# Three homes in turn for the weights of 24 expert blocks, with each weight group issued only when the group two ahead has landed

## The reference, cut to what matters

```python
# 4 groups x 8 experts, each token goes to the best group and to the best 2 experts in it
def expert_block(args):                       # one block of tokens, one expert e
    xe, e = args
    return (jax.nn.silu(xe @ w1[e]) * (xe @ w3[e])) @ w2[e]
# w1[e], w3[e]: 1024 x 512; w2[e]: 512 x 1024; 32 experts in each of 2 layers
```

## Time and profile before

| | |
|---|---|
| median of 3 runs | 1816.01 us (1814.39 to 1816.27) |
| profiled execution | 1816.97 us |
| its span | 1815.2 us |
| PE busy | 1743.2 us (96%) |
| DVE, ACT, POOL busy | 538.1, 525.4, 167.9 us |
| DMA, HBM read | 468.15 MB, 261 GB/s over the span |
| SP's queue of weights | 450.98 MB |

### The profile page before, as it was taken

One profiled execution on the slowest core, in us unless ns is written; L12 is line 12 of the kernel. 1 busy time (PEld: TensorE's weight loads), 2 busy tenths in 40 slices (PEclk: granted clock), 3 DMA queues, 4 the chain that ended last, 5 costly groups with the idle time before them and its releaser, 6 DMA issues.

```text
span 1815.2 us, 23627 instructions
## 1 busy us (share of the span) xinstructions
PE 1743.2 (96%) x9138; PEld 831.6 (46%) x9138; DVE 538.1 (30%) x987; ACT 525.4 (29%) x941; POOL 167.9 (9%) x208
## 2 busy tenths in 40 slices
PE   8999999999999999989999999999999999989898
PEld 4555777455533333333334434685433333333333
DVE  2154555422422231312223004212243232222223
ACT  3245342523322222222223004513432222222213
POOL 2000351110100000000002000320100000000000
PEclk9999999999999999999999999999999999999999
DMA  7210100363499999999994123106399999999995
GB/s 198 93 47 1 48 2 2 109 242 139 150 410 396 421 422 420 421 421 422 420 382 151 48 79 107 47 0 251 123 358 360 421 421 421 421 421 422 421 421 220
DMA packets 98391, 466.48 MB, mean 257 GB/s; under 512 B 23423, under 2 KB 25583, under 8 KB 49178
## 3 DMA queue, kind: packets, MB, share of 16 engines
q1 hardware_dynamic: 87392, 450.98, 62.1%
q0 software_dynamic: 4608, 7.92, 1.2%
q10 hardware_dynamic: 6330, 6.71, 1.2%
HBM read 468.15 MB, written 6.29 MB: 261 GB/s over the span
## 4 chain that ended last, share of the span: by engine, by line
PE 72%; DMA 23%; DVE 2%; ACT 2%; issue 1%; SPq 0%; DVEq 0%; ACTq 0%
PE ps L1132 65%; DMA W<-in_moe_w 23%; PE ps L1341 2%; PE ps L1874 1%; PE ps L1837 1%; ACT MK L900 0%; PE ps L1576 0%; PE ps L1278 0%; PE ps L1145 0%; PE ps L1368 0%; PE ps L1789 0%; DVE gcs L2296 0%; DVE gsn L2327 0%; PE ps L1748 0%; PE ps L1740 0%
## 5 line engine op out<-in xcount | busy, mean ns | idle before, releaser
L1132 PE MATMUL ps<-W,xgT 128*64 128x512 f32 x1984 | 458.2, 599 | 11.6 <-DMA W<-in_moe_w 10.1
L1132 PE MATMUL ps<-HT,W 128*128 128x512 f32 (+2 forms) x896 | 333.9, 533 | 2.8 <-DVE HT L2014 1.4
L1132 PE MATMUL ps<-W,act 128*64 128x512 f32 x992 | 236.6, 611 | 28.4 <-DMA W<-in_moe_w 28.4
L1132 PEld LDWEIGHTS ps<-W,xgT 128*64 128x64 f32 x1984 | 131.2, 136 | 259.8 <-issue 239.7
L1132 PEld LDWEIGHTS ps<-HT,W 128*128 128x128 f32 (+1 forms) x896 | 165.8, 188 | 159.0 <-issue 146.7
L1088 ACT ACTIVATE ysb<-ps 32x512 f32<-32x512 f32 x248 | 146.0, 589 | 262.2 <-PE ps L1132 260.1
L2455 DVE TENSOR_TENSOR XT<-ps,XT 128x512 f32<-128x512 f32 x248 | 159.8, 686 | 170.4 <-PE ps L1132 170.4
L2449 DVE TENSOR_TENSOR act<-ps,sl 128x256 f32<-128x256 f32 x64 | 27.0, 422 | 473.0 <-ACT sl L1081 473.0
L1077 ACT ACTIVATE hs<-ps 128x512 f32<-128x512 f32 x64 | 38.2, 597 | 429.2 <-PE ps L1132 429.2
L1132 PE MATMUL ps<-spread,ysb 64*128 64x256 f32 x992 | 139.8, 401 | 2.7 <-DVE ysb L2475 1.7
L1132 PEld LDWEIGHTS ps<-W,act 128*64 128x64 f32 x992 | 65.8, 139 | 155.3 <-issue 112.9
(11 more groups left out here) (430 smaller groups left out, 1584.8 us busy)
## 6 DMA issues: line engine op xcount, KB each, us to landing
W<-in_moe_w SPq DMA_DIRECT2D x372, 1024.0 KB, 17.5
W<-in_od_w_in SPq DMA_DIRECT2D x6, 2048.0 KB, 8.8
W<-in_ev_w_in SPq DMA_DIRECT2D x3, 2048.0 KB, 7.9
W<-in_xa_wq SPq DMA_DIRECT2D x2, 2048.0 KB, 8.8
W<-in_xa_wo SPq DMA_DIRECT2D x2, 2048.0 KB, 12.8
WY<-in_moe_w SPq DMA_DIRECT2D x4, 1024.0 KB, 8.6
hrows<-hk ACTq DMA_DIRECT2D x8, 512.0 KB, 5.0
HT<-in_moe_w SPq DMA_DIRECT2D x4, 1024.0 KB, 7.7
```

The source lines that it names most:

```text
L1132: return te.matmul(o, l, r, start=first, stop=last)
```

## The change

Three things, and one that makes room for them.

1. **The third place becomes a home.** In the first 12 pairs of a layer (`TURNED = 3 * ROUNDS = 12`), block n uses home n mod 3, where home 2 is HT, WX and WY. Blocks 24 and 25 then stand in homes 0 and 1, and from pair 13 on the old loop with two homes runs.
2. **The order is that of use.** A3 B3, A4 B4, C3, A5 B5, C4, and so on to A24 B24, C23, A25 B25, C24; then the old order. A home is reused after three blocks, so that the wait for PE is for block n-3.
3. **A hold.** Before it issues a group of blocks 4 to 24, SP also waits until the group two ahead of it in this order has landed. A4 waits for B3, the group just before it, and B4 waits for C2, which has long landed. The C groups of blocks 5, 8, ... 23 have no hold, and nothing from A25 on has one.
4. **Semaphores.** Two are needed for home 2 (`third_in`, `second_in`). `brow_in` is counted in `par_in`, and `mem_in` and `gup_in` in one `late_in`, so that PE waits once for 19 small loads where it waited for 14 and then for 5. PE reads the number of pairs after pair 12 and not after pair 1, and adds what the turned part left out to six landing counts.

```diff
-                def up(b, i, readers=0):
+                def up(b, i):
...
+                def hold(signals, place, use):
+                    sp.sem_inc(s["go"], 1)
+                    if place == 2:
+                        sp.wait_ge(s[signals[1]], use * 32 + 32 * (1 + 2 * ROUNDS * L))
+                    else:
+                        sp.wait_ge(signals[0][place], use * 32 + (32 + pairs * 32))
+
+                def turned_up(n, place, use=None):
+                    e = bass.ds(sp.value_load(bei[0:1, bass.ds(n, 1)], min_val=0, max_val=NX - 1), 1)
+                    w1, w3 = (a[k][L][e][0].rearrange("(p k) n -> p k n", p=P) for k in ("moe_w1", "moe_w3"))
+                    for half, signal in enumerate(("hh_half", "hh_done")):
+                        sp.wait_ge(s[signal], n + (pairs * 2 + L))
+                        if use is not None and half:
+                            hold((w2_in, "second_in"), (place + 1) % 3, use[0])
+                        elif use is not None:
+                            hold((w13_in, "third_in"), (place + 2) % 3, use[1])
+                        if place < 2:
+                            up_half(L, place, e, half)
+                        else:
+                            k4 = slice(4 * half, 4 * half + 4)
+                            sp.dma_start(HT[:, k4, :], w1[:, k4, :]).then_inc(s[("extra_in", "third_in")[half]], 16)
+                            sp.dma_start(WX[:, k4, :], w3[:, k4, :]).then_inc(s[("extra_in", "third_in")[half]], 16)
+
+                def turned_down(n, place, use=None):
+                    e = bass.ds(sp.value_load(bei[0:1, bass.ds(n, 1)], min_val=0, max_val=NX - 1), 1)
+                    sp.wait_ge(s["y_done"], n + (pairs * 2 + L))
+                    if use is not None:
+                        hold((wa_in, "extra_in"), (place + 1) % 3, use)
...
-                up(0, 2, readers=1)
-                up(1, 1)
-                down(0, 2, readers=1)
-                down(1, 1)
-                up(1, 2)
-                with sp.Fori(3, trips) as i:
+                turned_up(3, 0)
+                with sp.Fori(1, 2 * ROUNDS) as r:
+                    for q in range(3):
+                        turned_up(r * 3 + (q + 1), (q + 1) % 3, (r + ((q - 1) // 3), r))
+                        turned_down(r * 3 + q, q, r if q < 2 else None)
+                turned_up(2 * TURNED + 1, 1)
+                turned_down(2 * TURNED, 0)
+                with sp.Fori(TURNED + 1, trips) as i:
...
-                            pe.wait_ge(s["par_in"], 16 * (len(PARAMS) - 1))
+                            pe.wait_ge(s["par_in"], 16 * (len(PARAMS) - 1 + 5))
                             te.transpose(ps[:, 2, 0:NPAR], prow[:, :], ident[0:NPAR, 0:NPAR])
-                            pe.wait_ge(s["brow_in"], 16 * 5)
...
-                pair_of_blocks(0, first=True)
-                pair_of_blocks(1, extra=True)
+                for i in range(3):
+                    m = 2 * i
+                    pair_of_blocks(i, ((m % 3, m // 3), ((m + 1) % 3, (m + 1) // 3)), ((m - 1) % 3, (m - 1) // 3), first=i == 0)
+                with pe.Fori(1, ROUNDS) as r:
+                    for p in range(3):
+                        m = 2 * p
+                        pair_of_blocks(r * 3 + p, ((m % 3, (r, m // 3)), ((m + 1) % 3, (r, (m + 1) // 3))), ((m - 1) % 3, (r, (m - 1) // 3)))
+                for place in range(2):
+                    for landing in (wa_in, w13_in, w2_in):
+                        pe.sem_inc(landing[place], 32 * (TURNED - 2 * ROUNDS))
+                pair_of_blocks(TURNED, former=(2, 2 * ROUNDS - 1))
                 pe.wait_ge(s["plan_v"], PLAN_V * (L + 1))
                 trips = pe.value_load(nit[0:1, 0:1], min_val=MIN_TRIPS, max_val=MAX_TRIPS)
-                with pe.Fori(2, trips - 1) as i:
+                last = pe.value_load(nit[0:1, 1:2], min_val=MIN_TRIPS - 1, max_val=MAX_TRIPS - 1)
+                with pe.Fori(TURNED + 1, last) as i:
                     pair_of_blocks(i)
```

More of the change, by code:

```diff
@@ L1846, in add_tiles, with landed, up @@
                     ins.then_inc(s["added"], 1)
-                def up(b, i, between=None, extra=False):
+                def landed(use, per):
+                    return use[0] * (2 * per) + per * (use[1] + 1) if isinstance(use, tuple) else (use + 1) * per
+                def up(b, i, at, between=None):
+                    place, use = at
                     if b == 0:
                         pe.wait_ge(s["xgT_in"], i + (pairs + (L + 1)))
-                    first, third = (HT, WX) if extra else (W8[EXPERT[b]], W8[EXPERT[b] + 1])
-                    if extra:
-                        pe.wait_ge(s["extra_in"], 96 * (L + 1))
+                    first, third = (HT, WX) if place == 2 else (W8[EXPERT[place]], W8[EXPERT[place] + 1])
+                    if place == 2:
+                        pe.wait_ge(s["extra_in"], landed(use, 32) + 32 * 2 * ROUNDS * L)
                     else:
-                        pe.wait_ge(wa_in[b], (i + 1) * 32 + pairs * 32)
+                        pe.wait_ge(wa_in[place], landed(use, 32) + pairs * 32)
                     for k in range(KD):
@@ L1860, in up @@
                             between(k)
-                        if k == 4 and not extra:
-                            pe.wait_ge(w13_in[b], (i + 1) * 32 + pairs * 32)
+                        if k == 4 and place == 2:
+                            pe.wait_ge(s["third_in"], landed(use, 32) + 32 * 2 * ROUNDS * L)
+                        elif k == 4:
+                            pe.wait_ge(w13_in[place], landed(use, 32) + pairs * 32)
                         x = xgT[:, b, k, :]
@@ L1875, in turn_hidden, with down @@
                     ins.then_inc(s["hs_turned"], 1)
-                def down(b, i, bank=6, between=None, extra=False):
+                def down(b, i, at, bank=6, between=None):
+                    place, use = at
                     k0 = i * 2 + (pairs * 2 + b)
                     pe.wait_ge(s["act_in"], k0 + 1)
-                    second = WY if extra else W4[EXPERT[b] + 2]
-                    if not extra:
-                        pe.wait_ge(w2_in[b], (i + 1) * 32 + pairs * 32)
+                    second = WY if place == 2 else W4[EXPERT[place] + 2]
+                    if place == 2:
+                        pe.wait_ge(s["second_in"], landed(use, 32) + 32 * 2 * ROUNDS * L)
+                    else:
+                        pe.wait_ge(w2_in[place], landed(use, 32) + pairs * 32)
                     if bank == 6:
@@ L1909, in next_rows, with pair_of_blocks @@
                         turn_rows(i * 16 + (pairs * 16 + 16))
-                def pair_of_blocks(i, first=False, extra=False, last=False):
-                    up(0, i, extra=extra, between=(lambda k: slots() if k == 4 else None) if first else None)
+                def pair_of_blocks(i, at=None, former=None, first=False, last=False):
+                    at = at or ((0, i), (1, i))
+                    up(0, i, at[0], between=(lambda k: slots() if k == 4 else None) if first else None)
                     if not first:
-                        down(1, i - 1)
+                        down(1, i - 1, former or (1, i - 1))
@@ L1925, in moe @@
-                pair_of_blocks(1, extra=True)
+                    down(0, i, at[0], between=lambda: next_rows(i, first, last))
+                for i in range(3):
[5 more added lines that the diff above has]
+                        pair_of_blocks(r * 3 + p, ((m % 3, (r, m // 3)), ((m + 1) % 3, (r, (m + 1) // 3))), ((m - 1) % 3, (r, (m - 1) // 3)))
```

54 lines of the change are left out of this document (26 added, 28 removed).

## The result

| | before | changed |
|---|---|---|
| median (all runs) | 1816.2 us (1813.8 to 1819.3, 16 runs) | 1820.9 us (1817.9 to 1825.7, 16 runs) |
| ratio to before | | 1.0029, 95% interval 1.0022 to 1.0035 |
| profiled execution, span | 1817.0, 1815.2 us | 1822.8, 1821.0 us |

The change costs 4.7 us. 1814.4 us and a chance of 0.45 for "no change that can be measured" were forecast; the time is within the range (1805 to 1824 us), but on the other side of the kernel before.

A forecast was written before the change was run, and what follows sets the result against it. The prediction took the DMA loads to bound both expert stages; -7.0 (idle time removed) + 5.4 (gap at A4) + 0 (later holds) = -1.6 us, from 1816.0 to 1814.4 us, range 1805 to 1824 us.

The forecast's parts named there:

- The bound: Both expert stages: DMA loads set the pace, 31.1 us a pair against PE's 28.1; A31's landing sets the stage's end.
- Removed: Early in each stage: three homes end the queue's idle time, 1.7 us in layer 0 and 5.3 in layer 1, 7.0 gained.
- the bill: DMA time from A3 to A31: 83 steps of 5.0 us and 14 gathers of 1.1 us, with either kernel.
- Added once a stage: At A4, which waits for B3: the queue runs empty, 2.7 us lost in each stage, 5.4 in all.
- The upper bound of 3.1: At A4: the most one stage could lose, 3.1 us, if the second piece needs 7.5 us from its issue.
- Added at each later hold: Some 110 holds after A4: 4.8 us of cover still in flight, so 0 lost; ends -0.03 and +0.2 us each.
- The rest: Order of use, PE's count reads and semaphore additions, longer loops' register arithmetic, single wait for small loads: priced at nothing.
- The uncovered hold: Blocks 4 to 24, 56 holds a stage: each leaves a gap, 1826 or 1837 us; 23% together with moved gaps.
- The short queue that keeps the engines together: Held part: laggard engines gain bandwidth, some 4 us a stage, 1806 us; 32% together with no gap at A4.
- the 26.2 against 26.1 GB/s of an engine alone: Argument against the short queue: a lagging engine moves 26.2 GB/s with half idle, 26.1 with all working; gains 0.6%.
- The gap isn't there: At A4: wait passed early or gap takes in the gather, 1809 to 1811 us; 32% together with engines kept together.
- Three homes change nothing: Idle gaps only move to a later block, the 5.4 us stay: 1821 us; 23% together with the uncovered hold.

The follow-up runs named there:

- e15: Changed kernel, holds kept, with gathers of pairs 2 to 15 fetching rows 0 to 127, all valid: 1826.5 us, 1.0057 of the kernel before.
- e2: Changed kernel with all waits of the holds taken out, real gathers: 1814.7 us, 0.9995 of the kernel before.
- e17: Changed kernel without any hold, real gathers, run a second time: 1814.9 us, 0.9992 of the kernel before.
- e16: Kernel before, with gathers of pairs 2 to 15 fetching rows 0 to 127, all valid, run a second time: 1821.7 us, 1.0031 of the kernel before.
- e1: Changed kernel with the hold taken from A4 alone, all other holds kept: 1815.3 us, 0.9997 of the kernel before.
- e5: Changed kernel with the gather of pair 2 issued only after A4 has landed: 1820.1 us, 1.0025 of the kernel before.
- e4: The changed kernel itself, run once more: 1820.7 us, 1.0026 of the kernel before.
- e13: Changed kernel, holds kept, with gathers of pairs 2 to 15 fetching no valid row: 1823.3 us, 1.0037 of the kernel before.

## Why the prediction was wrong

**The bound: right.** What shifts A31 shifts the end; PE had time to spare. From A31's landing to HT's issue in layer 1 every trace takes 376.4 to 378.4 us, and the differences go with PE's clock ahead of HT; from A31's landing in layer 1 to the end it is 34.2 us in all of the 16-pair traces but e15 (35.3).

**"Removed", 7.0 us gained: this step failed.** It measured 1.2 us (e2, e17). The gaps in the queue did go; what was wrong is what they are worth. Two faults in the term, and a loss outside it:
- In layer 1 the bill counted a gather twice. It took 1.1 us for each of 14 gathers "with either kernel" and then called all of the 10.3 us step beyond 5.0 idle. But POOL issued a gather at 1380.85 us that landed 4.0 us later, inside that step (1382.8 to 1393.1 us), and its 1.1 us had been billed already:

```profile
1380.85 1.01 POOL L670 DMA_INDIRECT xg<-hrows,idc  x1 [0.85 <-POOL idc L667]
```

  Idle time to be won: 5.3 - 1.1 = 4.2 us. From WX to A31 the kernels without holds gain just that, 4.3 and 4.5 us.
- In layer 0 time was won and paid back. Without holds (e2) the group that lands at 559.8 us in the old kernel landed at 559.2, and the next one, at 566.0, landed at 564.1. These last 1.3 us aren't the idle time: in both kernels a load of instructions passed in this step, and only the old one's is longer for it (6.2 us against 5.0). Then the gathers issued about 571 and 599 us made their steps 6.3 us long each in e2, where the old kernel's are 5.5 and 5.3 us (581.5 - 576.0 and 611.8 - 606.5), and one step with an instruction load took 5.9 us (585.3 to 591.2). By 638 us nothing was left (638.5 against 638.0); e17, which has no such step, kept 1.2 us from WX to A31. With full gathers the old kernel's two steps are 6.0 and 6.2 us (e16). So after the idle time of layer 0 a half-empty gather cost the old kernel some 0.5 us, and a full one its whole price. That some engines have few rows and catch up meanwhile is my reading; no row shows the engines one by one.
- Outside the term: the stores' wait, 2.0 us more with the changed order, was in no step. By the traces 4.5 to 5.7 us are won from WX on and 2.0 given back ahead of it, which leaves 2.5 to 3.7; the medians say 1.2. The difference of 1.3 to 2.5 us is no more than one profiled execution can stray from its median, and stays unexplained.

**"Added once a stage", 5.4 us lost: right in kind and close in size.** e1 says 5.4 to 5.6. By the layers it was wrong: 2.7 each was forecast, and from WX on the changed kernel loses 3.4 to 4.9 us in layer 0 against the kernels without the gap and 1.5 to 2.1 in layer 1. (For layer 0 the prediction took its time from the earlier trace rows; by the old order that second group is B4, and B3 stands in its place in the changed one.) The upper bound of 3.1 was too low where a gather falls into the filling of the queue: A4 took 10.7 and 10.3 us there, 7.7 with the gather moved (e5). In layer 1 the gather, issued at 1356.21 us, 3.5 us ahead of A4, makes neither B3's step nor A4's longer, so that its 1.1 us are hidden: 2.8 - 1.1 = 1.7. The prediction drew on the Trainium skill's page "DMA: Bandwidth & Descriptors" (Anatomy of one DMA) for a fixed cost of 2.0 us; that section is on DMAs issued from GpSimd, and these are SP's. The runs have 2.8 us for the empty queue, landing to issue included.

**"Added at each later hold", 0: right with the real gathers.** It is e1 against e2 (0.7 us), and 46.7 us per three blocks. The lower rate in the slices (411 against 421 GB/s) cost nothing; that the last engine's work sets the pace and the early ones wait for it fits, and so does that the held part of e15, with full gathers, moves 421 GB/s from 700 to 800 us, but no row shows the engines one by one. With empty gathers it isn't 0: 5.0 us a run lie in steps with instruction loads.

**"The rest", 0:** not shown; no kernel undid it alone. It thought of the longer loops' register arithmetic and not of their instructions, which have to be loaded: 57 loads on q8 where 45 were. As far as it can be read, in steps with a load and no gather beside it, they cost little with the real gathers: such steps are 2.1 us too long in all in the kernel before, 1.7 and 1.0 in e2 and e17, 2.6 and 2.8 in the changed kernel and e4. The stores' later landing may hang on the loads or on something else of the changed program.

**The rivals.** The uncovered hold: falls with the real gathers (e1 against e2). The short queue that keeps the engines together: half of it is there. SP's queue in 1786.8 to 1805.8 us of the changed kernel, after A31's landing:

```profile
q1 hardware_dynamic: 656, 4.71, 59.5%
```

4.71 MB are left where 3.83 were the earlier trace rows, so by the prediction's reading the engines are 0.9 MB closer together, and the stage is no shorter for it, as the 26.2 against 26.1 GB/s of an engine alone had said. The gap isn't there: falls; it is the loss. "Three homes change nothing" named 1821 us, the time that came, with another mechanism: it had the idle gaps move on, but in e2 and e17 the seven slices behind each stage's first are all at 420 and above: the gaps are gone. What didn't come is their worth.

So the sum was 7.0 - 5.4 = 1.6 us gained; measured, 1.2 - 6.0 = 4.8 us lost. 5.8 of the 6.4 us of error is the first term. That 1820.9 us lies in the range is no merit of the sum: the range reached there for rivals that fell.

The changed kernel without holds (e2, and again e17) isn't faster than the kernel before by more than the measurement tells: 0.9995 and 0.9992, with upper ends of 1.0004 and 1.0001. A change that keeps the removed idle time and brings WX's start back was not tried.

## What to carry to other kernels

When idle time of a queue is priced by the length of a step, first take out what else passed in that step, small gathers included; otherwise it is billed both as work and as idle time. A hold on an issue was free here, with the real gathers, while a whole group was still in flight, and cost 2.8 us where nothing was; what mattered is which group the wait names, not how many waits there are. Work from another queue that falls just ahead of the refilling of an empty queue can cost more than it does elsewhere. And a loop that is unrolled or made longer has instructions to load through the same DMA engines: count the packets of the instruction queues in both profiles before putting it at nothing.

## What the runs showed of the hardware

- A gather of 128 rows of 4 KiB costs a DMA-bound stage 1.2 us a pair whether about half or all of its rows are valid (31.1 us a pair in both, with 7.92 and 16.22 MB in its queue over the run), and nothing when none is (29.9).
- A 2 MiB group issued into an empty queue needed 7.7 to 7.8 us in six cases (four with no gather's rows beside it, in e5 and e13, two with a half-empty gather issued 3.5 and 4.1 us before it), and 10.3 and 10.7 us with a half-empty gather issued 2.2 to 2.4 us before it. With a full gather issued 0.7 and 2.2 us before it, it needed 9.2 and 8.7 us (e15).
- The mean rate of the 16 engines can be 2.4% lower (411 against 421 GB/s over 100 us) with groups landing at the same pace.
- The wait for four stores of token rows beside HT's 2 MiB took 10.5 to 10.8 us in twelve stages of the old order and 10.5 to 12.8 us in twenty-two of the changed one, though the code there is the same.
- Of 139 steps between 2 MiB groups in which a 16 KB load of instructions passed, 38 were over 5.5 us, of 1650 without one 3; in the mean a step with a load was 0.85 us too long in the old order, 0.3 in the changed one with holds and 0.1 without.
